# Two edits in a two-block transformer kernel: the window attention's inverted totals spread by transfers, and block 1's gate columns in the rotary key's tile

## The chip, the cores and the metric

The program runs on one core of one Trainium2 chip. The metric is the device time of one execution in microseconds. The unchanged kernel took 3802.32 us, the median of three runs (3802.03, 3802.32 and 3806.3).

## What is computed

The input is 512 positions of 1024 channels, float32. Block 1 has two layers: a feed-forward part, a mixer of three groups (latent attention with 4 heads, a bidirectional gated recurrence called mLSTM with 4 heads, a Fourier group), a second feed-forward part and a gate. Block 2 has two layers as well: a mixer of window attention (8 query heads), a gated linear recurrence (HGRN2, 4 heads) and a delta-rule recurrence (4 heads), and a feed-forward part. Two places of it matter here.

In block 1 the mixer's input projection gives, among others, the rotary key and the 16 gate columns of the mLSTM:

```python
IN_SPLITS = (MLA_Q_LORA, MLA_KV_LORA, MLA_ROPE_DIM, MLSTM_WIDTH, MLSTM_WIDTH, MLSTM_WIDTH, 4 * MLSTM_HEADS, FNET_WIDTH)
u = rmsnorm(h, mix_norm[i]) @ w_in[i]
c_q, c_kv, k_rope, m_x, m_v, m_o, m_if, f_in = split_cols(u, IN_SPLITS)
```

In block 2 the window attention divides by a total for each head and position, before or after the product with v:

```python
p = jnp.exp(scores - m)
denom = p.sum(axis=-1, keepdims=True) + jnp.exp(sink - m)
out = jnp.einsum('bnhgqk,bnkhd->bnqhgd', (p / denom).astype(v.dtype), vb)
```

## The kernel before

**Data.** Activations stand with channels on partitions and the 512 positions along the row. Every large product is made of three TensorE passes over fp32r halves (`split_products`, L334 to L336: high times high, low times high, high times low). The weights come through a ring: SP loads 512 KB into `raw` (L400), ACT rounds it to the high half (L412), DVE takes the difference as the low half (L422), PE uses it. One column tile is 8 x 3 matmuls of 128x512.

**Stages.** A stage is a block of five instruction streams, one for each engine, and the next stage starts behind a barrier. Inside, the order on each engine is that of the code, and semaphores tie the engines together.

**Block 1's projection** (`Project1`, with `Project`). Eleven column tiles: three for the query's latent, two for the key's, two each for the mLSTM's input and output gate, one with the rotary key twice (into `kr`), and one with the gate columns spread over 128 columns (into `kr_tmp`); then four items in which positions stand on partitions ("row part", whose results ACT and DVE copy at L1470 and L1477). DVE evicts each tile at L1554 with the norm's factor `R`, the reciprocal of L615. PE's row sums (L1433) wait for the first eviction. SP loads the next stage's `uq` and `ukv` behind the ring's items. ACT adds the gates' biases (L1537, L1538) and then copies its half of the row part.

**Block 2's mixer** (`mixer2`). Two programs are woven on each engine (`weave`): first the delta rule, `delta_*`, and second the window attention followed by the HGRN2 recurrence, `window_*` and `hgrn_*`. They take turns, one step of each, up to the next `yield`. So an instruction that waits holds up the other program on its engine too.

- The window attention leaves its unnormalised outputs in `yv[:, 0:4]`, two heads (64 partitions each) a tile, and the inverted totals in `inv_rows`, 8 rows of 512, one for each head, which ACT writes at L2572.
- Then follow 14 level steps of HGRN2 (`steps`): DVE makes differences (L2747, L2748), ACT exponentials (L2693), DVE products (L2760, L2761), PE small matmuls (L2629), DVE merges them under a mask (L2772). Beside them runs the delta rule's triangular inversion: POOL masks (L3030), PE L2839, L2847 and L2861, ACT L2929 and L2934, DVE L2991.
- Then come the outputs of HGRN2 (L2658 to L2665) and its head norm (`HeadNorms`: sums L2132, root L2138, reciprocal L2143, spreading L2147, scaling L2152), woven with four steps of the delta rule's state: PE L2889 and L2898, DVE L3000, PE L2902 and L2906, DVE L3007, ACT L2947.
- The inverted totals are spread to the heads' partitions by PE: `spread_totals` (L2599) multiplies `inv_rows` by a 0/1 matrix, and `scale_output` (L2603) multiplies `yv` by the result in PSUM. Both stand in the tail, twice two of the four tiles, among the steps of the head norm.

## Time and profile before

| | |
|---|---|
| median of three runs | 3802.32 us |
| profiled execution, its own time | 3797.43 us |
| its span | 3795.7 us |
| PE busy | 3683.5 us (97%) |
| DVE busy | 2212.1 us (58%) |
| ACT busy | 1297.3 us (34%) |
| POOL busy | 744.9 us (20%) |
| transfers | 345.40 MB, 91 GB/s on average |

The span is the time from the first to the last instruction in the profiled execution. The busy time of PE counts pipelined matmuls whose ends are modelled. A row of the timeline gives the start in us from the span's start, the duration of the merged rows, the engine, the line of the kernel, the tile written and the tiles read, the count, and in brackets how long the engine was idle before and what ended that. The tile `arena` is one large buffer in which most smaller ones lie. Layer 0 of block 1 has its projection from about 386 to 466 us, layer 0 of block 2 its mixer from about 2388 to 2594 us, and the second layers show the same sequence later.

### The profile page before, as it was taken

The numbers are of one execution on the slowest core, as the hardware profiler recorded it, in microseconds if no ns is written. First come the engines' busy times: TensorE is split into PE (matmuls) and PEld (weight loads), VectorE is DVE, ScalarE is ACT, GpSimd is POOL, SyncE is SP. The second block draws the span as 40 slices with busy tenths as digits, with TensorE's granted clock in tenths as the row PEclk, the third lists the DMA queues.
The fourth block names the chain that finished last, engine by engine and source line by source line (L and its number), as shares of the span: only waits on it lengthen the run. The fifth ranks groups of instructions, "written<-read, shape, count | busy, mean of one in ns | idle before, by whom it ended". The sixth has DMA issues, their size and how long they took to land. (4 is left out here: it accounts for less than half of the span.)

```text
span 3795.7 us, 41460 instructions
## 1 busy us (share of the span) xinstructions
PE 3683.5 (97%) x16570; PEld 2860.5 (75%) x16570; DVE 2212.1 (58%) x2936; ACT 1297.3 (34%) x1876; POOL 744.9 (20%) x448
## 2 busy tenths in 40 slices
PE   8999999999999999999999999999999999999999
PEld 6888744888878888546888876786888767867887
DVE  7655557655575555457755576565544556645444
ACT  3223235422242223334422344444222343543221
POOL 3432002244204330001434013120000020300000
PEclk9999999999999999999999999898999998989999
DMA  5443200444334443102444322002333220012332
GB/s 175 144 137 116 94 24 23 135 137 131 125 100 134 136 134 102 60 24 89 140 132 138 102 79 61 6 1 67 95 95 100 83 79 21 1 51 85 99 100 83
DMA packets 93087, 345.40 MB, mean 91 GB/s; under 512 B 10977, under 2 KB 11233, under 8 KB 92001
## 3 DMA queue, kind: packets, MB, share of 16 engines
q1 hardware_dynamic: 92896, 342.76, 28.2%
q8 instruction: 132, 2.16, 0.2%
q14 instruction: 59, 0.48, 0.0%
HBM read 340.62 MB, written 2.10 MB: 90 GB/s over the span
## 5 line engine op out<-in xcount | busy, mean ns | idle before, releaser
L412 ACT ACTIVATE w_hi<-raw 128x1024 fp32r<-128x1024 f32 (+2 forms) x540 | 558.5, 1037 | 1814.1 <-PE ps L336 1733.1
L334 PE MATMUL ps<-xs_hi,w_hi 128*128 128x512 f32 x2312 | 911.3, 394 | 2.5 <-DVE arena L1300 2.5
L336 PE MATMUL ps<-xs_hi,w_lo 128*128 128x512 f32 x2312 | 903.6, 391 | 0.0
L335 PE MATMUL ps<-xs_lo,w_hi 128*128 128x512 f32 x2312 | 903.4, 391 | 0.0
L422 DVE TENSOR_TENSOR w_lo<-raw,w_hi 128x1024 fp32r<-128x1024 f32 (+2 forms) x540 | 676.0, 1253 | 148.0 <-ACT w_hi L412 147.4
L334 PEld LDWEIGHTS ps<-xs_hi,w_hi 128*128 128x128 f32 x2312 | 436.3, 189 | 105.0 <-issue 14.9
L335 PEld LDWEIGHTS ps<-xs_lo,w_hi 128*128 128x128 f32 x2312 | 436.2, 189 | 93.8 <-issue 3.6
L336 PEld LDWEIGHTS ps<-xs_hi,w_lo 128*128 128x128 f32 x2312 | 436.2, 189 | 91.5
L334 PE MATMUL ps<-hd_hi,w_hi 128*128 128x512 f32 x1288 | 503.3, 391 | 1.5 <-DVE hd_lo L1037 1.5
L336 PE MATMUL ps<-hd_hi,w_lo 128*128 128x512 f32 x1288 | 501.2, 389 | 0.0
L335 PE MATMUL ps<-hd_lo,w_hi 128*128 128x512 f32 x1288 | 501.1, 389 | 0.0
L827 POOL TENSOR_SCALAR arena<-arena,parg 128x768 f32<-128x768 f32 x128 | 305.4, 2397 | 955.7 <-DMA arena<-in_ada 697.6
L1033 DVE TENSOR_TENSOR arena<-arena,ps 128x512 f32<-128x512 f32 x132 | 90.7, 687 | 355.4 <-PE ps L336 350.7
L334 PEld LDWEIGHTS ps<-hd_hi,w_hi 128*128 128x128 f32 x1288 | 241.7, 188 | 53.1 <-DVE hd_lo L1037 2.0
L335 PEld LDWEIGHTS ps<-hd_lo,w_hi 128*128 128x128 f32 x1288 | 241.8, 188 | 51.0 <-issue 1.0
L336 PEld LDWEIGHTS ps<-hd_hi,w_lo 128*128 128x128 f32 x1288 | 241.7, 188 | 50.2
L835 POOL TENSOR_TENSOR arena<-arena 128x768 f32<-128x768 f32 x112 | 224.5, 2004 | 9.6 <-POOL arena L833 0.6
L1028 DVE TENSOR_TENSOR arena<-ps,stream_rstd 128x512 f32<-128x512 f32 x132 | 91.2, 691 | 230.9 <-PE ps L336 230.5
L1059 DVE SCALAR_TENSOR_TENSOR arena<-ps,stream_rstd 128x512 f32<-128x512 f32 x96 | 66.4, 691 | 156.9 <-PE ps L336 156.1
L2190 POOL TENSOR_SCALAR arena<-arena,par 128x512 f32<-128x512 f32 x4 | 10.3, 2582 | 671.7 <-DVE arena L2392 671.3
L1062 DVE TENSOR_TENSOR stream<-stream,arena 128x512 f32<-128x512 f32 x144 | 112.3, 780 | 4.9
L334 PE MATMUL ps<-ys_hi,w_hi 128*128 128x512 f32 x256 | 101.4, 396 | 2.7 <-DVE w_lo L422 2.7
(480 smaller groups left out, 4624.0 us busy)
## 6 DMA issues: line engine op xcount, KB each, us to landing
raw<-in_ffn_gu SPq DMA_DIRECT2D x264, 512.0 KB, 3.8
arena<-in_ada SPq DMA_DIRECT2D x64, 768.0 KB, 5.7
raw<-in_ffn_dn SPq DMA_DIRECT2D x96, 448.0 KB, 3.3
raw<-in_in_t SPq DMA_DIRECT2D x60, 512.0 KB, 3.7
raw<-in_ffn_dn SPq DMA_DIRECT2D x48, 512.0 KB, 3.5
raw<-in_out SPq DMA_DIRECT2D x32, 512.0 KB, 3.8
raw<-in_pleg SPq DMA_DIRECT2D x16, 512.0 KB, 3.7
raw<-in_in_r SPq DMA_DIRECT2D x8, 512.0 KB, 3.9
```

The source lines that it names most:

```text
L334: T.matmul(bank, lhs_hi(k), rhs_hi(k), start=(first and k == 0), stop=False)
L335: T.matmul(bank, lhs_hi(k), rhs_lo(k), start=False, stop=False)
L336: mm = T.matmul(bank, lhs_lo(k), rhs_hi(k), start=False, stop=(last and k == kt - 1))
L412: A.activation(self.hi[:, n % HL, 0:size], raw[:, n % RAW, 0:size], ACT.Copy).then_inc(self.high_done, 1)
L422: V.tensor_tensor(self.lo[:, n % HL, 0:size], raw[:, n % RAW, 0:size], self.hi[:, n % HL, 0:size].bitcast(F32), ALU.subtract).then_inc(sel ...
L827: G.tensor_scalar(aw[:, e, :], aw[:, e, :], cond(k0 + e), None, ALU.mult).then_inc(self.scaled, 1)
L835: ins = G.tensor_tensor(a, a, aw[:, e, :], ALU.add)
L1028: V.tensor_tensor(gn[:, j % 2, :], ps[2 * (j % 2)][:, :], R[:, :], ALU.mult).then_inc(self.gate_read, 1)
L1033: V.tensor_tensor(hf[:, j % 2, :], gn[:, j % 2, :], ps[2 * (j % 2) + 1][:, :], ALU.mult).then_inc(self.up_read, 1)
L1059: V.scalar_tensor_tensor(out=tmp[:, o % 2, :], in0=ps[4 + o % 2][:, :], scalar=self.scales[o], in1=R[:, :], op0=ALU.mult, op1=ALU.mult).th ...
L1062: V.tensor_tensor(h[:, o, :], h[:, o, :], tmp[:, o % 2, :], ALU.add).then_inc(self.h_updated, 1)
L2190: G.tensor_scalar(cv[:, c, :], cx[:, c, 0:S], w_(0), None, ALU.mult).then_inc(self.tap, 1)
```

## The change

**Gate columns.** The rotary key is put once into its column tile, in columns 0 to 63, and the 16 gate columns take columns 64 to 79 of it; the separate gate tile goes, so that there are ten column tiles. DVE evicts the tile into `kr_tmp`. ACT copies its first 64 rows twice into `kr`. The gates now stand in rows 64 to 79, and four transfers of 4x512 bring them to rows 0 and 32 of two new buffers, `gate_rows`, whose first 32 rows DVE sets to zero at the stage's start. ACT waits for these transfers before it adds the biases, and before its copies of the row part.

**Inverted totals.** `spread_totals` and `scale_output` go. In their place SP issues eight transfers, one for each head, that copy a row of `inv_rows` to the 64 partitions of the head in `inv_of`, four buffers that hold other data before and after. DVE waits for all eight in the step i == 3 of the level loop and makes the four products there (`scale_outputs`). ACT's copy of U, which writes over `inv_of`, waits for them.

```diff
@@ -476,7 +476,6 @@
         for l in range(DEPTH):
             feed(t["ffn1_gu"], t["ffn1_dn"], l)
             pairs_of(t["in1_t"], l, 10)
-            columns(t["in1_g"][l, :, :], 1)
             columns(t["in1_r"][l, :, :], 4)
             pairs_of(t["out1"], l, DT)
             half = t["plep"][l, :, :].rearrange("p (k m) -> p k m", k=2)
@@ -1482,7 +1481,8 @@
 
 
         def __init__(self, st, l, m, x, source, space):
-            super().__init__(st, x, source, 11, S)
+            super().__init__(st, x, source, 10, S)
+            self.gates_moved = st.sem("gates_moved")
             cq, ckv = m[1], m[2]
             self.nq = Norm(st, "nq", [cq[:, k, :] for k in range(3)], [cq[:, k, :] for k in range(3)],
                            [col(l, c1, "q_norm", k) for k in range(3)], 384, space, ps[6][:, :])
@@ -1502,6 +1502,11 @@
             sp.wait_ge(self.copied, 1)
             sp.dma_start(uq.rearrange("p k m -> p (k m)"), t["uq"][self.l, :, :]).then_inc(self.next_landed, 16)
             sp.dma_start(ukv.rearrange("p k m -> p (k m)"), t["ukv"][self.l, :, :]).then_inc(self.next_landed, 16)
+            sp.wait_ge(self.spread, 1)
+            for g in range(2):
+                for d in range(2):
+                    r = HD + 2 * H * g + H * d
+                    sp.dma_start(gate_rows[g][32 * d:32 * d + H, :], kr_tmp[r:r + H, :]).then_inc(self.gates_moved, 16)
             sp.wait_ge(self.next_landed, 32)
 
         def pe_after(self, pe, j):
@@ -1511,7 +1516,7 @@
             if j == 7:
                 pe.wait_ge(self.row_rooted, 1)
                 self.nk.pe(pe)
-            if j == 10:
+            if j == 9:
                 pe.wait_ge(self.nq.rooted, 1)
                 pe.wait_ge(self.nk.rooted, 1)
 
@@ -1529,29 +1534,34 @@
                 if j == 6:
                     act.wait_ge(self.copied, 5)
                     self.nk.square(act)
-                if j == 8:
+                if j == 7:
                     self.nq.take_root(act)
                     self.nk.take_root(act)
             act.wait_ge(self.spread, 1)
-            for rows_, bias, r in ((gi, "i_bias", 0), (gf, "f_bias", 64)):
-                A.activation(rows_[0:32, :], kr_tmp[r:r + 32, :], ACT.Identity, bias=col(self.l, c1, bias)[0:32, :])
-                A.activation(rows_[32:36, :], kr_tmp[r + 32:r + 36, ::-1], ACT.Identity, bias=col(self.l, c1, bias)[32:36, :])
+            for half in (slice(0, HD), slice(HD, P)):
+                A.activation(kr[half, :], kr_tmp[0:HD, :], ACT.Copy)
+            act.wait_ge(self.gates_moved, 64)
+            for rows_, bias, r in ((gi, "i_bias", gate_rows[0]), (gf, "f_bias", gate_rows[1])):
+                A.activation(rows_[0:32, :], r[0:32, :], ACT.Identity, bias=col(self.l, c1, bias)[0:32, :])
+                A.activation(rows_[32:36, :], r[32:36, ::-1], ACT.Identity, bias=col(self.l, c1, bias)[32:36, :])
             self.act_rows(act, self.parts)
 
         def dve(self, dve):
             y, cq, ckv, kr, mx, mo, gi, gf, vz, uq, ukv = self.m
             dst = [cq[:, 0, :], cq[:, 1, :], cq[:, 2, :], ckv[:, 0, :], ckv[:, 1, :], mx[:, 0, 2:2 + S], mx[:, 1, 2:2 + S],
-                   mo[:, 0, :], mo[:, 1, :], kr, kr_tmp]
+                   mo[:, 0, :], mo[:, 1, :], kr_tmp]
             for j in range(self.count):
                 if j == 0:
                     ring.low(dve, self.n0 + HL)
                     V.memset(mx[:, :, 0:2], 0.0)
                     V.memset(mx[:, :, S + 2:S + 4], 0.0)
+                    for rows_ in gate_rows:
+                        V.memset(rows_[0:32, :], 0.0)
                     for i in range(2):
                         V.memset(vz[:, :, 3 * HD * i + HD:3 * HD * i + 2 * HD], 1.0)
                     self.dve_start(dve)
                 dve.wait_ge(ring.used, self.n0 + j + 1)
-                V.tensor_tensor(dst[j], ps[j % 4][:, :], R[:, :], ALU.mult).then_inc(self.spread if j == 10 else self.copied, 1)
+                V.tensor_tensor(dst[j], ps[j % 4][:, :], R[:, :], ALU.mult).then_inc(self.spread if j == 9 else self.copied, 1)
                 if j:
                     ring.low(dve, self.n0 + j + HL)
                 if j == 3:
@@ -1560,10 +1570,10 @@
                     self.nq.add(dve)
                 if j == 6:
                     self.nk.add(dve)
-                if j == 9:
+                if j == 8:
                     self.nq.invert(dve)
                     self.nq.dve_finish(dve)
-                if j == 10:
+                if j == 9:
                     self.nk.invert(dve)
                     self.nk.dve_finish(dve)
             for j in range(self.count, self.count + 4):
@@ -1591,6 +1601,7 @@
         return Space(HD_AT + DT * S, SPLIT - DT * S), Space(X_AT, REST_AT - X_AT)
 
     kr_tmp = arena[:, SPARE_AT:SPARE_AT + S]
+    gate_rows = [arena[:, SPARE_AT + (1 + g) * S:SPARE_AT + (2 + g) * S] for g in range(2)]
 
     def rotate(dve, order, x, turned, table, tmp):
 
@@ -2595,15 +2606,23 @@
                         V.reciprocal(w_inv, w_inv).then_inc(inv_ready, 1)
                     yield
 
-            def spread_totals(pe, j, bank):
-                T.matmul(ps[bank][:, :], pick_pair(8, j), inv_rows, start=True, stop=True).then_inc(inv_spread, 1)
-
-            def scale_output(dve, j, bank):
-                dve.wait_ge(inv_spread, j + 1)
-                V.tensor_tensor(yv[:, j, :], yv[:, j, :], ps[bank][:, :], ALU.mult).then_inc(y_scaled, 1)
+            inv_of = [WT[:, 0, :], WT[:, 1, :]] + [U[:, 2 * a:2 * a + 2, :].rearrange("p a c -> p (a c)") for a in range(2)]
+
+            @st.block.sync
+            def _(sp):
+                sp.wait_ge(inv_rows_ready, 1)
+                sp.wait_ge(y_copied, 8)
+                for j in range(4):
+                    for e, r in enumerate(heads_of):
+                        sp.dma_start(inv_of[j][r, :], inv_rows[2 * j + e:2 * j + e + 1, :].unsqueeze(1).to_broadcast([1, HD, S])) \
+                          .then_inc(inv_spread, 16)
+
+            def scale_outputs(dve):
+                dve.wait_ge(inv_spread, 128)
+                for j in range(4):
+                    V.tensor_tensor(yv[:, j, :], yv[:, j, :], inv_of[j], ALU.mult).then_inc(y_scaled, 1)
 
             def hgrn_pe(pe):
-                pe.wait_ge(inv_rows_ready, 1)
                 pe.wait_ge(pT_copied, 16)
                 pe.wait_ge(y_copied, 8)
                 for c in range(2):
@@ -2665,18 +2684,11 @@
                     mm = T.matmul(out[:, 3 * P:S], v_(3), diag[:, hd, 3, :], start=False, stop=True)
                     if e:
                         mm.then_inc(o_done, 1)
-                for j in range(2):
-                    spread_totals(pe, j, 2 + j)
                 yield
-                pe.wait_ge(y_scaled, 1)
                 hg_norm.pe_sums(pe)
-                pe.wait_ge(o_copied, 2)
-                for j in range(2, 4):
-                    spread_totals(pe, j, j - 2)
                 yield
                 yield
                 yield
-                pe.wait_ge(y_scaled, 2)
                 for c in range(2):
                     hg_norm.pe_spread(pe, c, 2 + c, 2)
                 yield
@@ -2736,6 +2748,8 @@
                         for c in range(2):
                             V.tensor_scalar(far[:, c, 0, :], kd[:, c, 0:P], et[:, c, 1:2], None, ALU.mult).then_inc(tail_ready, 1)
                             V.tensor_scalar(far[:, c, 1, :], qd[:, c, 3 * P:S], et[:, c, 2:3], None, ALU.mult).then_inc(tail_ready, 1)
+                    if i == 3:
+                        scale_outputs(dve)
                     if i < len(steps):
                         v, c = steps[i]
                         L = LEVELS[v]
@@ -2775,11 +2789,7 @@
                              .then_inc(lev_copied, 1)
                     yield
                 yield
-                for j in range(2):
-                    scale_output(dve, j, 2 + j)
                 yield
-                for j in range(2, 4):
-                    scale_output(dve, j, j - 2)
                 yield
                 hg_norm.dve_invert(dve, slice(0, S // 2))
                 yield
@@ -2935,6 +2945,7 @@
                          .then_inc(xt_ready, 1)
                     yield
                 act.wait_ge(u_done, 1)
+                act.wait_ge(y_scaled, 4)
                 for a in range(2):
                     A.activation(U[:, 2 * a:2 * a + 2, :].rearrange("p a c -> p (a c)"), ps[4 + a][:, :], ACT.Copy).then_inc(u_copied, 1)
                 act.wait_ge(w_done, 1)
@@ -3313,13 +3324,8 @@
     w = x["w_in"]
     o = np.cumsum([0, 384, 256, 64, 256, 256, 256, 16, 256])
     cq, ckv, kr, mx, mv, mo, mif, fin = [w[:, :, o[i]:o[i + 1]] for i in range(8)]
-    f["in1_t"] = tile_pairs(np.concatenate([cq, ckv, mx, mo, kr, kr], 2))
-    gates = np.zeros((L, D, P), np.float32)
-    for g in range(2):
-        for d in range(2):
-            r = 64 * g + 32 * d
-            gates[:, :, r:r + H] = mif[:, :, 8 * g + 4 * d:8 * g + 4 * d + 4]
-    f["in1_g"] = rows(gates)
+    rest = np.zeros((L, D, 48), np.float32)
+    f["in1_t"] = tile_pairs(np.concatenate([cq, ckv, mx, mo, kr, mif, rest], 2))
     f["in1_r"] = rows(np.concatenate([mv, fin], 2))
     uq = x["mla_w_uq"].reshape(L, 384, 4, 192)
     f["uq"] = rows(np.concatenate([uq[..., :128].reshape(L, 384, 512), uq[..., 128:].reshape(L, 384, 256)], 2))
```

The order on PE, at the end of block 2's mixer in layer 0 (L2665 is the last output matmul of HGRN2, L2889 and L2898 open a state step, L2132 is the head sums), before:

```order
L2665 MATMUL ps<-arena 64x128
L2599 MATMUL ps<-arena,consts 128x512 x2
L2889 MATMUL ps<-arena 128x64 x4
L2898 MATMUL ps<-arena 64x128 x4
L2132 MATMUL ps<-arena,consts 4x512 x2
L2599 MATMUL ps<-arena,consts 128x512 x2
L2902 MATMUL ps<-arena 64x64 x4
L2906 MATMUL ps<-arena 64x128 x4
L2889 MATMUL ps<-arena 128x64 x4
```

And in the changed kernel, whose lines are a few higher (L2684, L2899, L2908, L2143, L2912 and L2916 stand for L2665, L2889, L2898, L2132, L2902 and L2906):

```order
L2684 MATMUL ps<-arena 64x128
L2899 MATMUL ps<-arena 128x64 x4
L2908 MATMUL ps<-arena 64x128 x4
L2143 MATMUL ps<-arena,consts 4x512 x2
L2912 MATMUL ps<-arena 64x64 x4
L2916 MATMUL ps<-arena 64x128 x4
L2899 MATMUL ps<-arena 128x64 x4
```

The two pairs of L2599 are gone, and nothing else has moved. On DVE, in the level loop (L2991 is the inversion's update, L2747 and L2748 the differences of the fourth step), before:

```order
L2991 TENSOR_TENSOR arena<-arena,ps 128x512
L2747 TENSOR_TENSOR arena<-arena 128x128x2
L2748 TENSOR_TENSOR arena<-arena 128x128x2
L2760 TENSOR_TENSOR arena<-arena 128x128x2
L2761 TENSOR_TENSOR arena<-arena 128x128x2
L2772 COPY_PREDICATED arena<-consts,ps 128x256 x2
```

And in the changed kernel (L3002 is the update, L2623 the four products):

```order
L3002 TENSOR_TENSOR arena<-arena,ps 128x512
L2623 TENSOR_TENSOR arena<-arena 128x512 x4
L2761 TENSOR_TENSOR arena<-arena 128x128x2
L2762 TENSOR_TENSOR arena<-arena 128x128x2
L2774 TENSOR_TENSOR arena<-arena 128x128x2
L2775 TENSOR_TENSOR arena<-arena 128x128x2
L2786 COPY_PREDICATED arena<-consts,ps 128x256 x2
```

The products stand ahead of the step's differences now. In the tail DVE loses them, before:

```order
L3000 TENSOR_TENSOR arena<-arena,ps 128x2x64 x2
L2603 TENSOR_TENSOR arena<-arena,ps 128x512 x2
L3007 SCALAR_TENSOR_TENSOR arena<-arena,ps 128x64 x2
L2603 TENSOR_TENSOR arena<-arena,ps 128x512 x2
L3000 TENSOR_TENSOR arena<-arena,ps 128x2x64 x2
L2143 RECIPROCAL arena<-arena 4x256
```

And in the changed kernel (L3011, L3018 and L2154 stand for L3000, L3007 and L2143):

```order
L3011 TENSOR_TENSOR arena<-arena,ps 128x2x64 x2
L3018 SCALAR_TENSOR_TENSOR arena<-arena,ps 128x64 x2
L3011 TENSOR_TENSOR arena<-arena,ps 128x2x64 x2
L2154 RECIPROCAL arena<-arena 4x256
```

Between two state steps DVE has only the recurrence's own updates left.

## Rows read from the trace of the kernel before

**Rows 1.** The page, part 1: busy us, share of the span, instructions.

```profile
PE 3683.5 (97%) x16570; PEld 2860.5 (75%) x16570; DVE 2212.1 (58%) x2936; ACT 1297.3 (34%) x1876; POOL 744.9 (20%) x448
```

**Rows 2.** Waits of PE: total us, times, longest us.

```profile
PE ps L2889 <- DVE arena L3007: 8.0, 6, 2.4
```

**Rows 3.** Timeline of DVE, projection of layer 0: start us, us, engine, line, tile, idle before.

```profile
433.43 0.69 DVE L1554 TENSOR_TENSOR arena<-ps,stream_rstd 128x512 f32<-128x512 f32 x1 [3.97 <-PE ps L336]
438.87 0.69 DVE L1554 TENSOR_TENSOR arena<-ps,stream_rstd 128x512 f32<-128x512 f32 x1 [3.06 <-PE ps L336]
```

**Rows 4.** Timeline of DVE and PE, start of that projection (columns as above).

```profile
392.89 0.55 DVE L1551 MEMSET arena<- 128x256 f32 x2
393.64 3.35 DVE L615 RECIPROCAL stream_rstd<-arena 128x512 f32<-128x512 f32 x1 [0.20 <-ACT arena L610]
...
397.78 1.05 PE L1433 MATMUL ps<-consts,stream_squares 128*128 128x1 f32 x8 [0.31 <-DVE arena L1554]
```

**Rows 5.** Timeline of SP and ACT, end of that projection, and `in_ukv`'s landing.

```profile
449.22 0.43 SPq L1504 DMA_DIRECT2D arena<-in_ukv  x1
...
449.47 0.72 ACT L1538 ACTIVATE arena<-arena,par 4x512 f32<-4x512 f32 x1
466.12 1.57 ACT L1470 ACTIVATE arena<-ps,rowsum 128x256 f32<-128x256 f32 x4 [15.93 <-PE ps L336]
...
DMA to landing us min/median/max: 8.1/8.8/9.4
```

**Rows 6.** ACT and SP, a landing, and a windows row ending in clock, DMA share, GB/s.

```profile
2477.25 0.59 ACT L2572 ACTIVATE arena<-ps 8x512 f32<-8x512 f32 x1
...
8.77 0.47 SPq L706 DMA_DIRECT2D positions<-in_pos  x1
...
parg<-in_parg SPq DMA_DIRECT2D x1, 10.0 KB, 1.7
...
452.00:456.00 4.00, 4.00 (x19) 3.30 (x19) 1.06 (x2) 0.00 (x0) 0.00 (x0) 1.00 0.99 416
```

**Rows 7.** Timeline of DVE and PE, first turns of block 2's level loop.

```profile
2482.52 0.68 DVE L2722 TENSOR_TENSOR arena<-arena 128x512 f32<-128x512 f32 x1
2498.46 0.69 DVE L2991 TENSOR_TENSOR arena<-arena,ps 128x512 f32<-128x512 f32 x1 [1.11 <-PE ps L2839]
2502.52 0.69 DVE L2991 TENSOR_TENSOR arena<-arena,ps 128x512 f32<-128x512 f32 x1 [0.82 <-PE ps L2839]
...
2514.49 1.11 PE L2629 MATMUL ps<-arena 64*128 64x64 f32 x16 [0.15 <-DVE arena L2772]
```

**Rows 8.** Line 2748: ns min/median/max, first and last start.

```profile
L2748 DVE TENSOR_TENSOR arena<-arena x28: 410/419/1318, 2487.0 to 3321.0; 128x256 f32<-128x256 f32 x28
```

**Rows 9.** Timeline of PE, ACT and DVE, end of block 2's mixer, layer 0.

```profile
2567.38 1.98 PE L2599 MATMUL ps<-arena,consts 8*128 8x512 f32 x4
2570.53 0.66 PE L2889 MATMUL ps<-arena 64*128 64x64 f32 x8 [1.16 <-DVE arena L3007]
2572.17 3.06 PE L2132 MATMUL ps<-arena,consts 128*4 128x512 f32 x4
2575.16 1.98 PE L2599 MATMUL ps<-arena,consts 8*128 8x512 f32 x4
2580.25 1.12 PE L2889 MATMUL ps<-arena 64*128 64x64 f32 x8 [0.39 <-DVE arena L3007]
...
2568.12 1.15 ACT L2127 ACTIVATE arena<-arena 128x512 f32<-128x512 f32 x2
2575.26 0.68 ACT L2138 ACTIVATE arena<-ps,consts 4x512 f32<-4x512 f32 x1 [4.70 <-PE ps L2132]
...
2578.17 1.73 DVE L2143 RECIPROCAL arena<-arena 4x256 f32<-4x256 f32 x1
```

**Rows 10.** Windows of that stretch: PE, PEld, DVE, ACT, POOL busy, then granted clock.

```profile
2579.00:2595.00 16.00, 11.85 (x77) 7.21 (x74) 7.23 (x16) 1.76 (x5) 0.00 (x0) 0.50 0.00 0
2597.00:2600.00 3.00, 3.00 (x8) 1.23 (x7) 2.96 (x5) 3.00 (x7) 0.00 (x0) 0.76 0.36 37
```

## The prediction

> **What bounds the kernel.** I read the page's busy shares first: PE is busy for 97% of the span [rows 1], so nearly every microsecond taken off PE's queue counts, and an edit elsewhere counts only where PE waits. Then PE's waits by line: they are small, and one of the larger, 8.0 us in all, is the state matmul of L2889 waiting for DVE's state update L3007 [rows 2]; it lies in the stretch that the change touches. Then the timelines of two places, the projection of block 1 and the mixer of block 2. Both layers of each block show the same pattern, so each cost is worked out for one layer and doubled.
>
> **Edit 1, the gate columns.** Block 1's projection has one column tile less. A tile is 24 matmuls, and two tiles' evictions stand 438.87 - 433.43 = 5.44 us apart, with DVE idle for PE before each [rows 3]: PE sets that pace. Two layers give **-10.9 us**. The tile's split on ACT and DVE and one 512 KB load go too, off the path.
>
> What it adds: two memsets of 32x512 on DVE ahead of the reciprocal L615. DVE waited only 0.20 us there, and PE's row-sum matmuls waited 0.31 us for the eviction behind the reciprocal [rows 4], so what exceeds 0.20 us reaches PE. Two memsets of 256 columns took 0.55 us together [rows 4]; at 512 columns they lie between that and 1.1 us, I take 0.95. That is +0.75 us a layer, **+1.5 us** in all, with ends +0.7 and +1.8.
>
> At the end of the projection ACT now copies the rotary key twice and then waits for four small transfers, which SP issues behind `in_ukv`; behind ACT's wait stand the gate activations and L1470. `in_ukv` is issued at 449.22 and lands 8.1 to 9.4 us later, at 458.6 at the latest [rows 5]. The four issues end by 451.6 (0.47 us each [rows 6]); with 1.7 us for a small transfer [rows 6] and the queue ahead they land by about 460. The four activations take 2.9 us (four of 0.72) and end at 463; ACT is idle for 15.93 us until L1470 at 466.12, when PE ends [rows 5]. Cover 3 us, cost **0**; what the transfers are later than that counts twice. Edit 1 is -10.9 + 1.5 = **-9.4 us**.
>
> **Edit 2, the tail of block 2's mixer.** PE loses four spreading matmuls a layer (L2599, in two pieces of 1.98 us), and DVE the four products that followed them. These products stood ahead of the state update in DVE's order, so PE waited another 1.16 us. From the start of the first piece to the next state matmul are 2570.53 - 2567.38 = 3.15 us [rows 9]. All of it goes: L3007 is then free as soon as its own matmuls are done, long before. What is late next: L2889 and L2898 start at 2567.4 and take 1.64 us, to 2569.0; the head sums L2132 need ACT's squares, which end at 2568.12 + 1.15 = 2569.27, about the same time. L2132 takes 2.99 us in the trace (2572.17 to 2575.16) and would now end at 2572.1 instead of 2575.2. Then come ACT's root (0.68 us) and DVE's reciprocal, which began only at 2578.17, since the second pair of products stood ahead of it; it can now begin at 2572.8. Behind it comes the update on which the state matmul of 2580.25 waited [rows 9]. That matmul moves forward by 5.3 us, and by up to one more if PE, without its 1.16 us of idle, keeps the higher clock in L2132; after it the order and the waits stay as they were, at granted clock 0.50 (1.2 GHz) in either case [rows 10]. I take **-5.6 us** a layer; the ends are 3.1, if only the first piece counts, and 6.4.
>
> **Edit 2, the level loop.** The four products move to the fourth turn of the loop (i == 3), between L2991 and L2747. One 128x512 product from SBUF took 0.68 us [rows 7], four 2.7 us. DVE has 0.82 us of idle behind that turn (before 2502.52), and from there DVE and PE go in step: at 2514.49 PE waits for DVE's L2772 [rows 7]. So 2.7 - 0.8 = **+1.9 us** of it reaches PE, if the data have landed. Between 1.5 and 2.8 us is open, since a product may fall beside a POOL instruction. L2748, the same instruction 28 times, takes 0.41 us or up to 1.32 [rows 8]. The Trainium skill (SBUF — State Buffer, Who interferes with whom) says that a VectorE instruction with two SBUF inputs and a GpSimd instruction that reads SBUF block each other whole; by this rule, with which the spread in L2748 agrees, the moved products cost up to 0.9 us more a layer than the old ones, which read PSUM.
>
> **Edit 2, the transfers.** This is the term that decides. SP can issue once the inverted totals stand in their rows, at 2477.25 + 0.59 = 2477.84 [rows 6]. Eight transfers copy one row of 2 KB each to 64 partitions: 8 x 64 x 2048 B = 1.05 MB. DVE comes to the products at 2498.46 + 0.69 = 2499.15 [rows 7]; 1.7 us is the least landing [rows 6], so 19.6 us are left for the bytes. They are hidden at 53 GB/s or more.
>
> No row shows a transfer that reads SBUF, or one whose bytes all come out of one partition. The rows bound it from far apart. A load into 128 partitions runs at 416 GB/s with the engines 0.99 busy [rows 6]: at that rate 2.5 us. The same row is 3.25 GB/s for each partition: if one gives no more, 323 us. And it is 416 / 16 = 26 GB/s for each of the 16 engines: 40.3 us. I take the last, an estimate. All eight sources lie in eight neighbouring partitions, so nothing spreads the reads as the 128 partitions of that row do, and the full rate asks a single partition for 128 times what it is seen to take; while 3.25 GB/s would assume that a partition is worked at its limit in that row, where the engines are.
>
> The Trainium skill (SBUF — State Buffer, Door 1: The DMA port swizzle) says that the rate depends on how many of 16 ports the partitions reach, and gives 27.6 GB/s for partitions 0 to 3. By it four transfers read through one port and then four through another, 38 us as an estimate, and the forecast would be 4.6 us less. No run here shows it yet.
>
> Landing is then 2477.84 + 1.7 + 40.3 = 2519.8, and DVE waits 20.7 us in its fourth turn. Behind the wait stand the evictions and updates of both recurrences, and PE waits for them. The shift is 20.7 + 2.7 - 0.8 = 22.6 us. PE comes back at the lower clock level, as it runs at 0.50 where it is little fed and is back at 0.76 on average only in the window of 2597 to 2600 [rows 10]; I add 1.3 us (0 to 3). With the tail's -5.6: **+18.3 us** a layer, +36.6 in two.
>
> **Sum.** -9.4 + 36.6 = +27.2 us. Against the profiled execution's own 3797.4 us (span 3795.7 and 1.7 around it) that is 3824.6; the median of the runs, 3802.3, lies 4.9 us higher, so the forecast for it is **3829.5 us**.
>
> **Rival A, the transfers are hidden** (faster). The transfers run at 53 GB/s or more and land before 2499. For it: sixteen engines take part, and SP and the queue are otherwise idle there. Against it: every byte comes out of eight partitions. Then a layer is +1.9 - 5.6 = -3.7, two -7.4, and the sum -9.4 - 7.4 = -16.8: **3785.5 us**. It decides from the landing: by 2499.15 in layer 0. The Trainium skill (DMA: Bandwidth & Descriptors, Where 436 GB/s comes from) lets the fabric's 435 GB/s bind for SBUF to SBUF, which would mean this rival; its two pages oppose each other here.
>
> **Rival B, they land within the loop but late.** Each microsecond behind 2499.15 costs two. At 37 GB/s they land at 2507.6 and the two edits cancel: 3802; at 45 GB/s (23.3 us, landing 2502.8) the wait is 3.7 us and the time 3785.5 + 7.4 = 3793.
>
> **Rival C, slower than one engine's share.** At 20 GB/s the bytes take 52 us, 12 more a layer: 3854.
>
> **Rival D, the gates' transfers land late** (both rates): a delay of 5 us beyond what I took for them exceeds the 3 us of cover and adds 4 us in two layers to any case.
>
> **Chances.** Forecast as worked out 0.50; A 0.34; B 0.10; C 0.06; D within each. Three runs of this kernel tell about 0.2% (8 us) from no change. Faster than 3794.7 is A and a part of B: 0.38. Within 0.2% is a narrow band of B: 0.04. Slower 0.58. The forecast's own range is 3819 to 3838 (tail 3.1 to 6.4, clock 0 to 3, share 26 to 27.6 GB/s). For 8 in 10 the range has to hold A as well: from 3781, A with the tail's upper end, to 3838.
>
> **What would show it.** In the changed profile: ten evictions of 5.44 us a layer in block 1's projection; the row sums' wait at about 1.1 us; L1470's copies right behind PE's end, or behind a landing (D). In block 2: the time from issue to landing of the last of the eight transfers, 40 us (forecast) or under 19 (A); DVE's idle time before the first product, 21 us or none; loop turns else as before; and in the tail no DVE product ahead of L3007, and the state matmul of 2580.25, 12.9 us behind the last output matmul (2567.38) before, about 7 us behind it. The forecast is wrong if that landing is under 20 us, and edit 1 is wrong if the projection's PE stretch is not 9 to 10 us shorter in two layers.

## The result: slower by 16 us

The changed kernel takes **3816.5 us** (median; 3810.7 to 3818.2), the kernel before 3800.2 us beside it: ratio 1.004, 95% interval 1.0027 to 1.0053, that is 15 us (10 to 20) slower. The forecast was slower, by 27 us, at 3829.5: the measured time lies 2.5 us below the forecast's own range of 3819 to 3838 and inside the wide one that starts at 3781. The profiled executions are 18.1 us apart in span (3813.8 against 3795.7).

The changed kernel's line numbers differ by a few: L1564 was L1554, L1432 was L1433, L2583 was L2572, L2648 was L2629, L2761 was L2747, L2786 was L2772, L2849 was L2839, L2899 was L2889, L2143 was L2132, L2154 was L2143, L3002 was L2991, L3011 was L3000, L3018 was L3007. New are L1509 (the gates' transfers), L1559 (the memsets), L2617 (the transfers of the totals) and L2623 (the products).

**Where the time went.** The table follows the same DVE instructions through both traces: each entry is the start of one in the changed kernel less its start in the kernel before. The difference of two neighbouring lines is what the stretch between them cost.

| mark (time in the kernel before) | changed less before, us |
|---|---|
| start of block 1's projection, layer 1 (1492) | -6.1 |
| totals ready in block 2's mixer, layer 0 (2478) | -11.1 |
| end of the level loop (2544) | +8.8 |
| first state update of the tail, L3011 (2556) | +5.7 |
| behind the tail's third step (2588) | -1.2 |
| behind the output projection's start (2618) | +0.9 |
| ahead of the loop of layer 1 (3260) | +3.3 |
| end of the loop of layer 1 (3337) | +23.2 |
| behind the tail's third step, layer 1 (3370) | +16.3 |
| behind the mixer of layer 1 (3400), and from there on | +18.2 |

Ahead of block 2's mixer 11.1 us are gained. Each level loop costs 19.9 us. From the loop's end to the third step of the tail 10.0 us come back in layer 0 and 6.9 in layer 1, and 2.1 and 1.9 of them are lost again up to the marks of 2618 and 3400.

The page's first line on the changed kernel, beside [rows 1]: PE is busy 20.5 us less, while the span grew by 18.1, so PE idles more.

```profile
span 3813.8 us, 41350 instructions
PE 3663.0 (96%) x16506; PEld 2850.0 (75%) x16506; DVE 2207.6 (58%) x2936; ACT 1297.0 (34%) x1878; POOL 739.1 (19%) x448
```

PE's waits by line (total, times, longest). The first row was not among them before; the line that stood high, the state matmul [rows 2], is at 8.9 us:

```profile
PE ps L2648 <- DVE arena L2786: 34.9, 4, 17.2
PE ps L2849 <- ACT arena L2944: 12.6, 12, 2.6
PE ps L2899 <- DVE arena L3018: 8.9, 4, 2.4
```

One step further back, DVE's timeline in the fourth turn of the loop, layer 0 (start, length, instruction, idle before it and what ended it), and PE's first row behind it. DVE reached the products at 2487.5 and stood until the transfers had landed:

```profile
2486.84 0.69 DVE L3002 TENSOR_TENSOR arena<-arena,ps 128x512 f32<-128x512 f32 x1 [0.56 <-PE ps L2849]
2504.74 2.50 DVE L2623 TENSOR_TENSOR arena<-arena 128x512 f32<-128x512 f32 x4 [17.21 <-DMA arena<-arena]
2509.93 1.97 PE L2648 MATMUL ps<-arena 64*128 64x64 f32 x16 [17.21 <-DVE arena L2786]
```

The transfers themselves, all sixteen, from the view of their line (issue time on SP in ns: least, median, most; first and last start; who waited; issue to landing of one). The first is issued at 2466.80 and the products start at 2504.74: 37.9 us for 1.05 MB. SP is held 4.4 us by most of the issues, where one of the rows before took 0.47 [rows 6]:

```profile
L2617 SPq DMA_DIRECT2D arena<-arena x16: 479/4436/4779, 2466.8 to 3287.2; - x16
  DVE arena L2623: 34.4, 2
DMA to landing us min/median/max: 6.9/16.8/17.6
```

Block 1's projection, layer 0, answers to [rows 4]. The two memsets took 1.02 us, and PE's row sums waited 1.02 us in place of 0.31:

```profile
392.95 1.02 DVE L1559 MEMSET arena<- 32x512 f32 x2
398.51 1.05 PE L1432 MATMUL ps<-consts,stream_squares 128*128 128x1 f32 x8 [1.02 <-DVE arena L1564]
```

Right behind that the granted clock of TensorE fell to about its lower level (0.50 is 1.2 GHz), which it had not done before. By windows (PE, PEld, DVE, ACT, POOL busy and instructions, granted clock, DMA share, GB/s), the changed kernel:

```profile
396.00:400.00 4.00, 2.98 (x18) 2.31 (x17) 3.96 (x4) 1.32 (x2) 0.00 (x0) 1.00 0.01 4
400.00:402.00 2.00, 2.00 (x7) 1.52 (x6) 1.93 (x3) 0.00 (x0) 0.00 (x0) 0.53 0.29 84
402.00:404.00 2.00, 2.00 (x7) 1.62 (x6) 0.00 (x0) 0.00 (x0) 0.00 (x0) 0.61 0.89 248
```

and the kernel before:

```profile
400.00:402.00 2.00, 2.00 (x11) 1.65 (x10) 1.19 (x2) 0.00 (x0) 0.00 (x0) 1.00 0.61 207
402.00:404.00 2.00, 2.00 (x11) 1.65 (x9) 0.00 (x0) 0.00 (x0) 0.00 (x0) 1.00 0.71 207
```

The fall does not come with every such wait. Seven of the profiled kernels have the memsets at this place, and in all of them PE waits 1.02 or 1.03 us there in both layers. In layer 0 the granted clock falls behind it in five (the changed kernel, `e1_gates`, `e5_hbm`, `e6_order`, `e8_none`) and stays at 1.00 in two (`e3_late`, `e7_end`); in layer 1 it stays at 1.00 in all seven. Where the wait is 0.30 or 0.31 us (the kernel before, `e2_totals`, `e4_memset`, `best`) it never falls there.

The gates' transfers were covered, as ACT's timeline at the end of that projection shows: behind the gate activations (the last ends at 458.76) it idled for 4.3 us until PE ended [rows 5].

```profile
455.83 0.73 ACT L1545 ACTIVATE arena<-arena,par 32x512 f32<-32x512 f32 x1 [10.36 <-DMA arena<-arena]
458.04 0.72 ACT L1546 ACTIVATE arena<-arena,par 4x512 f32<-4x512 f32 x1
463.07 1.57 ACT L1469 ACTIVATE arena<-ps,rowsum 128x256 f32<-128x256 f32 x4 [4.30 <-PE ps L336]
```

The tail of block 2's mixer, layer 0, answers to [rows 9]. From the end of the last output matmuls to the state matmul that was at 2580.25 are 2579.19 - 2573.06 = 6.13 us, where they were 2580.25 - 2567.38 = 12.87; DVE's reciprocal L2154 now waits for ACT alone and stands behind no product:

```profile
2573.06 0.66 PE L2899 MATMUL ps<-arena 64*128 64x64 f32 x8
2574.48 1.88 PE L2143 MATMUL ps<-arena,consts 128*4 128x512 f32 x4 [0.17 <-ACT arena L2138]
2577.11 1.74 DVE L2154 RECIPROCAL arena<-arena 4x256 f32<-4x256 f32 x1 [2.77 <-ACT arena L2149]
2578.78 0.36 DVE L3018 SCALAR_TENSOR_TENSOR arena<-arena,ps 128x64 f32<-128x64 f32 x2
2579.19 0.66 PE L2899 MATMUL ps<-arena 64*128 64x64 f32 x8 [2.02 <-DVE arena L3018]
```

### The profile page after: what moved, and what is told of

The parts are those of the page before. It is cut to its first block and busy times, and to the rows that moved or that the text cites. A ratio compares the mean times of both kernels' runs of the same rounds, so it can differ in the third digit from the quotient of the medians.

```text
span 3813.8 us, 41350 instructions
## 1 busy us (share of the span) xinstructions
PE 3663.0 (96%) x16506; PEld 2850.0 (75%) x16506; DVE 2207.6 (58%) x2936; ACT 1297.0 (34%) x1878; POOL 739.1 (19%) x448
## 5 line engine op out<-in xcount | busy, mean ns | idle before, releaser
L422 DVE TENSOR_TENSOR w_lo<-raw,w_hi 128x1024 fp32r<-128x1024 f32 (+2 forms) x538 | 668.0, 1243 | 145.5 <-ACT w_hi L412 144.9
```

The costliest lines, as they stand in the source:

```text
L422: V.tensor_tensor(self.lo[:, n % HL, 0:size], raw[:, n % RAW, 0:size], self.hi[:, n % HL, 0:size].bitcast(F32), ALU.subtract).then_inc(sel ...
```

## Experiments

Two theories stand against each other on the main term. **P:** a group of four neighbouring SBUF partitions has one way out of some 28 GB/s, all eight source rows lie in two such groups, and the wait for the landing is the whole loss. **Others:** a single partition is the limit, or any transfer from SBUF to SBUF, or the broadcast's descriptors, or the traffic beside the loop rather than its landing. The kernel before ran at 3799.9 to 3801.1 us beside them; an interval of a ratio is about 5 us to either side.

**The two parts apart.** `e1_gates` is the kernel before with the edits of block 1 alone, `e2_totals` with those of block 2's mixer alone (the diff of the change, split between them).

> The gate columns' part alone; block 2's mixer as before. By the ledger of the two traces (marks ahead of block 2's first mixer stand 11.0 us earlier in the changed kernel, and block 2's projection holds nothing of the change) this part is worth -11 us, -10.5 to -11.5. By the prediction's own term it is -9.4. Rival: part of these 11 us is a phase of the clock that the later stages give back; then it is -5 to -8. Block 1's projection: ten evictions a layer, DVE's two memsets 1.0 us, PE's wait for the row sums 1.0 us.

Measured 3787.1 us, ratio 0.9971 (0.996 to 0.9983), -11 us (6.5 to 15). That is the expected size, but the interval still holds the upper end of the rival.

> The transfers of the inverted totals alone; block 1 as before. If the two parts add up, +16.3 + 11 = +27 us (the prediction's term was +36.6). Eight transfers land 38 us behind the totals' rows, DVE idle 17 us before the first product in each layer, and the state matmul behind the last output matmul about 6 us behind it. Rival: in the changed kernel the two parts meet in the phase of the clock, and this one alone is under +22 or over +32.

Measured 3823.8 us, ratio 1.0058 (1.0046 to 1.0071), +22 us by the ratio and +24 by the medians, with 16.6 and 16.8 us of DVE's idle before the products. By the runs it is 17 to 27 us, which reaches from the rival to the +27 expected, and by the spans of the profiled executions it is 26.8 (3822.5 against 3795.7). The parts give -11 + 22 = +11, against 15 (10 to 20) for both together: they add up within what can be told.

**The rate by itself.** `m1_rates` has a stage behind the last output in which SP issues groups of transfers and waits for each:

```diff
+            for k in range(8):
+                put(k, row(k)).then_inc(landed, 16)
+            sp.wait_ge(landed, 144)
+            for k in range(8):
+                put(k, row(4 * (k % 2) + k // 2)).then_inc(landed, 16)
+            sp.wait_ge(landed, 272)
...
+                put(k, cst[0:8, 0:S].unsqueeze(1).to_broadcast([8, 8, S])).then_inc(landed, 16)
```

> The changed kernel with a stage of its own behind the last output, in which SP issues groups of transfers of one row of 2 KB to 64 partitions and waits for each group: one alone (131 KB), then groups of eight (1.05 MB). Sources of each group: partitions 0 to 7 one after another (as in the kernel); 0,4,1,5,2,6,3,7; partition 0 eight times; partitions 0,4,...,28 one each; each transfer from all of 0 to 7; each from 0,4,...,28; 64 partitions to 64; rows in HBM. Theory P (a group of four neighbouring partitions has one way out, some 28 GB/s): 37, 37 or 19 (if neighbours in the queue overlap), 37, 37 or less, 19, 6, 6, 5 us. Theory T (one partition's reads are the limit, whatever lies beside it): 37, 37 or 19, 37, 37 or less, 6, 6, 6, 5. Theory S (SBUF to SBUF is slow in itself): all 37 but the last 5. Theory I (a broadcast row costs by its descriptors): the last 37 too, the one of 64 partitions fast. The time of the kernel itself says nothing.

Windows of this kernel, each from the first issue of one group to that of the next (the last to about where the DMA engines fall idle), in the order of the expectation; columns as above, the length first:

```profile
3814.06:3820.37 6.31, 0.00 (x0) 0.00 (x0) 0.00 (x0) 0.00 (x0) 0.00 (x0) 0.50 0.60 21
3820.37:3858.28 37.91, 0.00 (x0) 0.00 (x0) 0.00 (x0) 0.00 (x0) 0.00 (x0) 0.50 0.83 28
3858.28:3881.93 23.65, 0.00 (x0) 0.00 (x0) 0.00 (x0) 0.00 (x0) 0.00 (x0) 0.50 0.79 44
3881.93:3921.98 40.05, 0.00 (x0) 0.00 (x0) 0.00 (x0) 0.00 (x0) 0.00 (x0) 0.50 0.85 26
3921.98:3943.09 21.11, 0.00 (x0) 0.00 (x0) 0.00 (x0) 0.00 (x0) 0.00 (x0) 0.50 0.74 50
3943.09:3965.53 22.44, 0.00 (x0) 0.00 (x0) 0.00 (x0) 0.00 (x0) 0.00 (x0) 0.50 0.43 47
3965.53:3974.98 9.45, 0.00 (x0) 0.00 (x0) 0.00 (x0) 0.00 (x0) 0.00 (x0) 0.50 0.41 111
3974.98:3981.79 6.81, 0.00 (x0) 0.00 (x0) 0.00 (x0) 0.00 (x0) 0.00 (x0) 0.50 0.67 154
3981.79:3988.80 7.01, 0.00 (x0) 0.00 (x0) 0.00 (x0) 0.00 (x0) 0.00 (x0) 0.50 0.66 148
```

Partitions 0 to 7 one after another take 37.9 us, to the microsecond what they take inside the kernel, so nothing beside them slows them. The sixth and seventh group decide: eight partitions per transfer take 22.4 us when they are neighbours (0 to 7) and 9.5 when they are four apart (0, 4, ..., 28). Both used the same number of source partitions and the same shapes, and a limit of one partition would have given both the same; a limit of SBUF to SBUF falls with the eighth group (64 partitions, 6.8 us), one of broadcast descriptors with the last (7.0). P stands. Its sizes were less exact: 19 us were expected for the sixth group and 22.4 came, 6 for the seventh and 9.5 came. The engines were busy for only 0.43 and 0.41 of the time in these two, against 0.83 in the second; no run tells what held them there. The third and fifth group show that transfers of one queue overlap when their sources lie in different groups, about two at a time. The Trainium skill (SBUF — State Buffer, Door 1: The DMA port swizzle) gives 27.6 GB/s for partitions 0 to 3; the fourth group agrees with 26. The fabric's 435 GB/s, which the Trainium skill (DMA: Bandwidth & Descriptors, Where 436 GB/s comes from) lets bind for SBUF to SBUF and by which rival A would have held, is not reached by such a source.

**Another order, another source.** `e6_order` issues the same eight transfers in the order 0, 4, 2, 6, 1, 5, 3, 7:

```diff
-                for j in range(4):
-                    for e, r in enumerate(heads_of):
+                for e, r in enumerate(heads_of):
+                    for a in range(2):
+                        for j in (a, a + 2):
```

> The changed kernel with the eight transfers issued in the order of source partitions 0, 4, 2, 6, 1, 5, 3, 7 in place of 0 to 7; same bytes, same products in the fourth turn. Theory (two groups of four partitions have a way out each, some 28 GB/s, and neighbours in the queue overlap; 0,4,1,5,... took 23.6 us by itself against 37.9): landing 23.6 us behind the first issue, so 2.9 us of DVE's idle stay in place of 17.2, the gain is 14.3 a layer and the time 3816 - 29 = 3787 (3781 to 3793). Rival (beside the kernel's own transfers and engines the order does not matter): 3816.

Measured ratio 0.996 (0.9947 to 0.9973), 3785 us by it (median 3782.1), inside the expected range. DVE's rows before the products in the two layers; 2.9 us of idle was foretold:

```profile
2489.25 2.50 DVE L2624 TENSOR_TENSOR arena<-arena 128x512 f32<-128x512 f32 x4 [2.89 <-DMA arena<-arena]
3271.19 2.52 DVE L2624 TENSOR_TENSOR arena<-arena 128x512 f32<-128x512 f32 x4 [2.28 <-DMA arena<-arena]
```

`e5_hbm` goes through HBM:

```diff
+                sp.dma_start(t["inv"][:, :], inv_rows).then_inc(inv_spread, 16)
                 sp.wait_ge(y_copied, 8)
+                sp.wait_ge(inv_spread, 16)
...
-                        sp.dma_start(inv_of[j][r, :], inv_rows[2 * j + e:2 * j + e + 1, :].unsqueeze(1).to_broadcast([1, HD, S])) \
+                        sp.dma_start(inv_of[j][r, :], t["inv"][2 * j + e:2 * j + e + 1, :].to_broadcast([HD, S])) \
```

> The changed kernel with another way for the totals: one transfer takes the eight rows (16 KB) to a scratch in HBM, and the eight transfers of one row to 64 partitions read it from there; the products stay in the fourth turn. Theory (SBUF's way out of few partitions is the limit; eight rows from HBM to 64 partitions each took 7 us in the group measured by itself): 2 us for the store and 7 for the rest, landed by 10 us behind the totals against the 20.8 us that DVE needs to its products. DVE's idle of 17.2 us goes to 0 and the time is 3816 - 2 x 18 = 3780 (3774 to 3788). Rival 1 (a transfer of one row to many partitions is slow beside the kernel's own work whatever its source): landing at 30 us or more, over 3798. Rival 2 (the round through HBM takes over 20 us): 3785 to 3800.

Measured 3777.3 us, ratio 0.9943 (0.9929 to 0.9956), as expected: with the landing out of the way this change is faster than the kernel before. SP's two rows and DVE's: the store has landed 1.5 us behind its issue, the eight issues take 5.76 us in all, and the products start without idle time.

```profile
2460.94 0.31 SPq L2614 DMA_DIRECT2D inv<-arena  x1
2462.48 5.76 SPq L2619 DMA_DIRECT2D arena<-inv  x8
2481.59 0.69 DVE L3004 TENSOR_TENSOR arena<-arena,ps 128x512 f32<-128x512 f32 x1 [1.18 <-PE ps L2851]
2482.19 3.39 DVE L2625 TENSOR_TENSOR arena<-arena 128x512 f32<-128x512 f32 x4
```

**Another place for the products.** `e3_late` keeps the slow transfers and moves the products to the tenth turn:

```diff
-                    if i == 3:
+                    if i == 9:
                         scale_outputs(dve)
```

> The changed kernel with one thing moved: the four products stand in the tenth turn of the level loop (i == 9) in place of the fourth, about 24 us later, by when the eight transfers (38 us from the totals) have landed. Theory (the wait for the landing is the whole loss): DVE's idle of 17.2 us before the first product goes to 0, the loop is 17 to 20 us a layer shorter, and the time is 3816 - 2 x 18 = 3780, 3775 to 3788, faster than the kernel before by 12 to 25 us. Rival 1 (the transfers or the products themselves disturb the loop, not their landing): under half of it comes back, over 3798. Rival 2 (the loop pays the products at their new place and the clock gives the rest back): 3790 to 3798.

Measured 3779.9 us, ratio 0.9944 (0.9932 to 0.9956), 37 us less than the changed kernel, as the theory had it. The wait is gone. But by the marks of the table the loop still costs 5.7 us in layer 0 and 2.8 in layer 1; in windows of layer 0, DVE is busy throughout, PE starves behind the products (2504.91 to 2508.29), and the granted clock falls:

```profile
2502.00:2507.00 5.00, 5.00 (x56) 4.74 (x53) 5.00 (x8) 1.89 (x4) 2.33 (x2) 1.00 0.00 0
2507.00:2512.00 5.00, 2.00 (x19) 1.84 (x18) 5.00 (x11) 1.60 (x3) 1.15 (x1) 0.88 0.00 0
2512.00:2517.00 5.00, 5.00 (x30) 4.88 (x30) 3.38 (x10) 1.23 (x2) 0.00 (x0) 0.50 0.01 3
```

So `e7_end` puts them behind the loop's last level copy:

```diff
-                    if i == 3:
-                        scale_outputs(dve)
...
+                    if i == len(steps) + 2:
+                        scale_outputs(dve)
                     yield
```

> The changed kernel with the four products behind the last level copy of the loop, at the end of its last turn. With the products in the tenth turn (3779.9 us) no wait for the landing was left, but PE had work for 2.0 of 5 us behind them, the granted clock fell to 0.50 and the loop ended 5.7 us later than without them; DVE had 7.7 us of idle behind the loop, and ACT overwrites the tiles that the totals landed in only 3.2 us behind the last level copy. Theory (a product inside the loop is paid by PE, and the clock with it; behind the loop it is free): 3 to 6 us a layer less than in the tenth turn, 3768 to 3774. Rival 1 (ACT and PE wait for the products at their new place): 3778 to 3786. Rival 2 (the clock drops at another place instead): 3776 to 3780.

Measured 3777.0 us, ratio 0.9943 (0.9928 to 0.9958): above the expected range, where rival 2 stood, and not told apart from the tenth turn. In the mixer it did what was expected. The products fit into DVE's idle time and ACT was not held up (it waited for PE, L2881):

```profile
2530.12 2.49 DVE L2623 TENSOR_TENSOR arena<-arena 128x512 f32<-128x512 f32 x4
2537.95 0.48 DVE L3011 TENSOR_TENSOR arena<-arena,ps 128x128 f32<-128x128 f32 x2 [5.34 <-PE ps L2899]
2533.42 1.09 ACT L2950 ACTIVATE arena<-ps 128x512 f32<-128x512 f32 x2 [6.16 <-PE ps L2881]
```

By the marks of the table the loop costs 0.1 us in layer 0 and nothing in layer 1, and the mixer of layer 0 with its tail -9.8 us. But 8.0 us of that go again between the marks of 2618 and 3260, where this version's text is that of the changed kernel. One window over block 2's second projection shows where, in the granted clock (third number from the end: 0.92 against 0.98); this version, then the kernel before:

```profile
3055.00:3164.00 109.00, 106.24 (x415) 76.67 (x414) 58.31 (x73) 37.79 (x46) 4.11 (x3) 0.92 0.17 49
```

```profile
3080.00:3182.00 102.00, 99.24 (x412) 73.25 (x412) 57.57 (x72) 37.63 (x45) 3.77 (x3) 0.98 0.18 52
```

`e8_none` leaves transfers and products out altogether: block 2's window outputs stay undivided, and only its time is of use.

> The changed kernel without the transfers and without the four products: block 2's window outputs stay undivided by their totals, which is left out of the computation. It is the floor of this part of the change. Theory (where the products stand behind the loop and the transfers have landed, neither costs anything): the time of the version with the products behind the loop, 3777.0, within 4 us. Rival 1 (the 1.05 MB beside the loop, or the four products and what waits for them, still cost something): 5 us or more below that, under 3772.

Measured 3775.2 us, ratio 0.9937 (0.9926 to 0.9949): the same as with the products behind the loop within what can be told. There 1.05 MB of transfers and the four products cost nothing that can be told.

**The memsets.** `e4_memset` is the changed kernel with them where DVE waits for PE anyway:

```diff
-                    for rows_ in gate_rows:
-                        V.memset(rows_[0:32, :], 0.0)
...
+                if j in (1, 2):
+                    V.memset(gate_rows[j - 1][0:32, :], 0.0)
```

> The changed kernel with the two memsets of the gate rows behind the second and third eviction of block 1's projection, where DVE waits for PE, in place of ahead of the reciprocal. In the changed kernel PE's wait behind that reciprocal was 1.02 us against 0.31, and the next evictions came 2.4 us late against the kernel before, of which 1.1 us are the memsets and the rest the granted clock, which fell to 0.53 and 0.61 there. Theory (the longer wait costs its length and a drop of the clock): PE's wait is 0.3 us again, no drop, and the time is 2 x 2.4 = 5 us less than the changed kernel's 3816, 3811. Rival 1 (only the memsets' own length counts): 2 us less, 3814. Rival 2 (the drop comes anyway, or its gain is given back by a drop elsewhere): 3816 within 2 us.

Measured 3810.9 us, ratio 1.0029 (1.0017 to 1.0042), 5.6 us less by the medians, where 5 were expected; the intervals of this and of the changed kernel overlap, so the runs do not tell this from rival 1. In the trace PE's row sums wait 0.30 us again and the clock does not fall:

```profile
399.49 1.05 PE L1432 MATMUL ps<-consts,stream_squares 128*128 128x1 f32 x8 [0.30 <-DVE arena L1562]
```

```profile
400.00:402.00 2.00, 2.00 (x12) 1.74 (x13) 1.96 (x4) 0.60 (x2) 0.00 (x0) 1.00 0.00 0
402.00:404.00 2.00, 2.00 (x11) 1.63 (x10) 1.85 (x3) 0.00 (x0) 0.00 (x0) 1.00 0.71 229
```

The expectation took the fall of the clock in both layers, and it comes in layer 0 alone. From DVE's first memset of the stage to ACT's first copy of the row part, the projection of layer 0 takes 73.3 us in the kernel before (392.82 to 466.12), 70.2 in the changed kernel (392.83 to 463.07) and 67.9 here (394.53 to 462.43); that of layer 1 takes 73.3, 68.6 and 67.9. So this version gains 5.4 us in each layer, and the changed kernel 3.1 and 4.7. The move is thus worth 3.1 us in the two projections together. The two spans differ by 5.0 us (3808.8 against 3813.8), but ahead of block 2's mixer by only 0.7; the other 4.3 arise in block 2, whose text is the same in both. The match with the 5 us expected is luck.

**Both moves together.** `best` is `e7_end` with the memsets of `e4_memset`.

> The changed kernel with both moves: the products behind the level loop (3777.0 us alone) and the memsets of the gate rows behind the second and third eviction (3810.9 in place of 3816.5 alone). If they add up, 3777.0 - 5.6 = 3771.4 (3768 to 3775), 29 us less than the kernel before. Rival (the clock falls at another place of block 2 and takes it back, as it took 8 us of the last one between the two mixers): 3775 to 3779.

Measured **3774.2 us**, ratio 0.9934 (0.9922 to 0.9947): 25 us (20 to 30) faster than the kernel before. This lies in the expected range and 0.8 us below the rival's, with runs from 3764.3 to 3777.0, so the two are not told apart. It is the lowest median, but its interval overlaps that of `e7_end`: that the memsets' move adds anything there is not shown.

## Why the prediction came out as it did

The sign and the mechanism were right: the landing of the transfers decides, at the rate of a few partitions and not at that of the engines [rows 6], and DVE's wait reaches PE whole. The sum was 9 us too high in the trace (+27.2 against +18.2), and the median missed the forecast's own range. (The low end of that range is 3821 by the three terms named with it, not 3819.) The step that was off most is the size of the landing: 7 of the 9 us. By the marks of the table, in two layers:

| term | forecast | trace |
|---|---|---|
| gate columns, all that comes ahead of block 2's mixer | -9.4 | -11.1 |
| level loops, with the wait | +47.8 | +39.8 |
| tails, to the marks of 2618 and 3400 | -11.2 | -12.9 |
| between the mixers | 0 | +2.4 |
| sum | +27.2 | +18.2 |

Another 4 us of the 13 between the medians come from the base. The forecast put the median 4.9 us above the profiled execution, as in the first three runs of the kernel before; in the changed kernel it lies 0.7 above.

- **Landing.** 1.7 + 40.3 us were taken, 37.9 came. DVE waited 17.2 us in each layer, not 20.7. That 26 GB/s came near was luck: the reason given was a sixteenth of the engines' rate, and `m1_rates` shows that the source's group of partitions sets it, since eight partitions four apart gave 111 GB/s. The landing that the prediction worked out from the Trainium skill (SBUF — State Buffer, Door 1: The DMA port swizzle), 38 us, agrees with 37.9. The upper share of 27.6 GB/s in the forecast's range comes from that section of the Trainium skill and not from a row; the second group of `m1_rates` bears it out with 28.
- **Loop.** 22.6 + 1.3 us a layer were taken, 19.9 came, 8.0 us less in two: 3.5 a layer from the landing and 0.5 from the rest. The lower clock behind the wait was there (L2648 took 1.97 us in place of 1.11), but cost little; DVE, not PE, sets the pace of this loop.
- **Products.** +1.9 with ends 1.5 and 2.8. Where nothing waits for a landing (`e5_hbm`) the loop costs 2.7 in layer 0: the ends held. All four took 3.39 us, one of them 1.58, with this POOL instruction beside them; behind the loop (`e7_end`), where POOL stood still, they took 2.49.

```profile
2483.43 1.60 POOL L3043 TENSOR_TENSOR arena<-arena,consts 128x512 f32<-128x512 f32 x1 [4.31 <-PE ps L2873]
```

- **Tail.** -5.6 was taken; from 2556 to 2588 it gave 5.7 + 1.2 = 6.9 us, and as much in layer 1, beyond the upper end of 6.4. L2143 ran at the higher clock (1.88 us in place of 3.06), which was counted only in part. Another 3.1 us were gained ahead of it in layer 0 and not foreseen: the matmuls behind the loop took 3.79 + 2.57 us where they had taken 4.74 + 4.71. The clock had fallen there in the kernel before and not in the changed one, as windows of the one and of the other show:

```profile
2548.00:2553.00 5.00, 5.00 (x36) 4.88 (x36) 0.00 (x0) 1.09 (x2) 0.00 (x0) 0.50 0.00 0
```

```profile
2553.00:2558.00 5.00, 4.53 (x43) 4.47 (x44) 1.10 (x3) 0.71 (x2) 0.00 (x0) 1.00 0.01 3
2558.00:2563.00 5.00, 4.27 (x67) 3.79 (x62) 0.49 (x2) 3.10 (x7) 0.00 (x0) 1.00 0.00 0
```

  The later start of this stretch is not the reason: `e8_none`, whose loop takes as long as before, gains the same 3.1 us there, and `e1_gates`, which keeps the spreading matmuls, does not. Nor did it all stay. Behind the tail, where the text is unchanged, the changed kernel loses 2.1 us in layer 0 and 1.9 in layer 1: in layer 0 the granted clock is 0.51 from 2608.8 to 2612.0, at the start of the output projection, where it had been 1.00 (2609.5 to 2612.7), and a matmul takes 0.63 us there in place of 0.39. In `e7_end` it does not happen. So the net of the tail is -7.9 in layer 0 and -5.0 in layer 1. That the stretch behind it would stay as it was, as the forecast took it, did not hold.

- **Gate columns.** -9.4 was forecast, -11.1 stood in the trace ahead of block 2's mixer, and -11 (6.5 to 15) came from `e1_gates`. But the projections themselves, from DVE's first memset to ACT's first copy of the row part, gave only 3.1 us in layer 0 and 4.7 in layer 1, 7.8 in all; by the prediction's own sign, 9 to 10 us, that is a miss. The tile was priced rightly: without the memsets ahead of the reciprocal (`e4_memset`, `best`) a projection gives 5.4 us, as against 5.44. The memsets were too: with them and no fall of the clock it gives 4.7 (layer 1 in all seven kernels that have them there, layer 0 in `e3_late` and `e7_end`), so they cost 0.7 where 0.75 was taken. The cover of the gates' transfers and PE's wait of 1.0 us at the row sums were right as well. What was missed is that the clock can fall behind this longer wait: where it does, in layer 0 of the other five, a projection gives 3.1, so the fall costs 1.6 us.

  The remaining 3.3 of the 11.1 us come outside the two projections, some 3 of them between the two, in text that the change does not touch, and why is open. The near match of 9.4 and 11.1 is luck to that extent. Seven profiled executions with the same text up to block 2's mixer stand between 10.8 (`e8_none`) and 16.9 us (`e5_hbm`) ahead of the kernel before there, so one trace alone tells this term to some 3 us.
- **Between the mixers** 2.4 us were lost, most of it to the clock in block 2's second projection, in text that the change does not touch. The same stretch costs nothing in `best`, 0.7 us in `e1_gates` and 8.0 in `e7_end`. What decides it stays open. It is also why the sum of good steps in one place is not the gain of the whole.
- **Rival A** gave 3785.5 for hidden transfers. The two versions in which they are hidden in the loop came to 3777 and 3780; 2 of the 6 to 8 us are the base (3802.3 in the forecast, 3800 beside these runs). The rest are the terms of block 1 and of the tail again: in the trace of `e5_hbm` -16.9 and -16.6 us, where -9.4 and -11.2 were forecast, less 4.3 lost between the mixers.

## What to carry to other kernels

Price a transfer by where its bytes come from, not only by how many there are: here a broadcast out of one group of four neighbouring partitions moved 26 to 28 GB/s, whatever the engines could do. Alternating between two groups raised it to 44, transfers that each read eight partitions four apart to 111, and reading the rows from HBM to 148. A wait put into the middle of an engine's queue costs its whole length in a loop where two engines go in step, so put the consumer behind the loop, where its engine idles anyway, rather than make the producer faster. And an addition ahead of an eviction on which PE waits may cost more than its own length: here 0.7 us, or 2.3 where the clock fell behind it, which it did in five traces of seven in one layer and in none in the other.

## What the hardware showed beyond that

- SP's issue instruction takes 4.4 us (the median of the sixteen) where the transfers are slow, against 0.6 for the same shapes out of HBM. That it is held until the queue ahead of it has room is a reading that no run tests. SP was at the eight issues of a layer for 26.5 us, so whatever it had to issue behind them would have waited too.
- A transfer from one group of partitions and the next from another overlap within one queue (23.7 us in place of 37.9 for the same bytes), though SP issued them all to the same queue.
- The store of 16 KB to HBM and its landing took 1.5 us, less than the least landing among the rows before (1.7, [rows 6]).
